# Halved norms of a two-block transformer kernel: narrower bank waits, another bank order, earlier evictions

## The reference

```
x = x + gt1 * mix                                           # "mix1"
x = x + gt2 * swiglu(modulate(x, norm2_g, sh2, sc2), ...)   # norm "n2", then "ffn1"
h = modulate_2(rmsnorm_2(x, g_ffn1), sh1, sc1)              # norm "nf1"
x = x + 0.5 * gt1 * swiglu_2(h, w_ffn1_in, w_ffn1_down)     # "ffn2"
proj = modulate_2(rmsnorm_2(x, g_mix), sh2, sc2) @ w_in     # norm "nm", then projections
x = x + gt2 * (y @ w_out)                                   # "mix2"
x = x + 0.5 * gt3 * swiglu_2(...)                           # norm "nf2", then "ffn3"
return rmsnorm_2(x, g_final)                                # norm "nfin"
```

## Time and profile before

| | us |
|---|---|
| median of 3 runs | 2013.97 (2013.62 to 2016.22) |
| the profiled execution | 2018.55 |
| its span, first to last instruction | 2016.7 |
| busy in the span: TensorE | 1956.7 (97%) |
| busy in the span: VectorE | 941.3 (47%) |
| busy in the span: ScalarE | 756.4 (38%) |
| busy in the span: GpSimd | 702.9 (35%) |

### The profile page before, as it was taken

How to read it: one execution, slowest core, us unless ns; L and a number is a source line. 1 busy time by engine, 2 the same in 40 slices (tenths; PEclk the granted TensorE clock), 3 DMA queues, 4 the chain that set the end, 5 groups by cost and what they waited for, 6 DMA issues and landing times.

```text
span 2016.7 us, 28119 instructions
## 1 busy us (share of the span) xinstructions
PE 1956.7 (97%) x11189; PEld 1572.3 (78%) x11189; DVE 941.3 (47%) x1465; ACT 756.4 (38%) x1298; POOL 702.9 (35%) x295
## 2 busy tenths in 40 slices
PE   7999999999999999999999999999999999999998
PEld 5788867888888888888888887656866788888886
DVE  2758668554444412544443255676875542323102
ACT  4553336543222213332221244445256442222212
POOL 1423301124444445244444523221421343444442
PEclk9989989999999999999999999999999999999999
DMA  7851100215444544244455522110311322333331
GB/s 315 301 208 43 48 7 22 84 50 167 146 137 148 183 134 140 76 154 146 135 172 187 172 72 78 46 53 22 94 43 32 94 85 94 94 95 103 94 94 63
DMA packets 61291, 223.38 MB, mean 111 GB/s; under 512 B 6928, under 2 KB 9232, under 8 KB 59536
## 3 DMA queue, kind: packets, MB, share of 16 engines
q1 hardware_dynamic: 60624, 219.70, 33.6%
q10 hardware_dynamic: 576, 2.43, 0.3%
HBM read 220.00 MB, written 2.10 MB: 110 GB/s over the span
## 4 chain that ended last, share of the span: by engine, by line
PE 88%; DVE 6%; ACT 2%; issue 2%; DMA 1%; SPq 0%; DVEq 0%; ACTq 0%
PE ps L450 77%; PE ps L1091 1%; DMA early_raw<-early 1%; DMA mod_w<-mod_w 1%; PE ps L1110 1%; DVE neg_max L1240 1%; PE ps L2539 1%; PE ps L2710 1%; PE ps L2731 1%; PE ps L1742 1%; PE ps L1101 0%; PE ps L2561 0%; PE ps L989 0%; PE ps L1011 0%; PE ps L2719 0%
## 5 line engine op out<-in xcount | busy, mean ns | idle before, releaser
L2119 POOL TENSOR_TENSOR w_lo<-raw,w_hi 128x1024 fp32r<-128x1024 f32 x262 | 635.5, 2426 | 1271.4 <-ACT w_hi L463 667.0
L450 PE MATMUL ps<-hh,w_hi 128*128 128x512 f32 (+1 forms) x1496 | 587.4, 393 | 8.5 <-DVE xT L1842 3.1
L450 PE MATMUL ps<-hl,w_hi 128*128 128x512 f32 (+1 forms) x1496 | 579.1, 387 | 0.0
L450 PE MATMUL ps<-hh,w_lo 128*128 128x512 f32 (+1 forms) x1496 | 578.8, 387 | 0.0
L450 PEld LDWEIGHTS ps<-hh,w_hi 128*128 128x128 f32 x1496 | 283.5, 190 | 74.9 <-issue 14.6
L450 PEld LDWEIGHTS ps<-hh,w_lo 128*128 128x128 f32 x1496 | 283.4, 189 | 58.1
L450 PEld LDWEIGHTS ps<-hl,w_hi 128*128 128x128 f32 x1496 | 283.7, 190 | 54.2
L2092 ACT ACTIVATE w_hi<-raw 128x1024 fp32r<-128x1024 f32 x126 | 133.7, 1061 | 469.5 <-PE ps L450 469.5
L516 DVE SCALAR_TENSOR_TENSOR mod_raw<-mod_raw,cond_ada 128x1024 f32<-128x1024 f32 x72 | 112.4, 1563 | 256.9 <-DMA mod_raw<-late 256.9
L450 PE MATMUL ps<-act_hi,w_hi 128*128 (+1 forms) x480 | 189.6, 395 | 0.0
L450 PE MATMUL ps<-act_hi,w_lo 128*128 (+1 forms) x480 | 189.6, 395 | 0.0
(11 more groups left out here) (494 smaller groups left out, 2691.6 us busy)
## 6 DMA issues: line engine op xcount, KB each, us to landing
raw<-stream SPq DMA_DIRECT2D x284, 512.0 KB, 3.6
mod_raw<-late SPq DMA_DIRECT2D x72, 512.0 KB, 4.6
early_raw<-early SPq DMA_DIRECT2D x32, 512.0 KB, 6.0
mod_w<-mod_w SPq DMA_DIRECT2D x8, 1024.0 KB, 20.1
xT<-xT SPq DMA_DIRECT2D x2, 1024.0 KB, 6.0
xT<-xT ACTq DMA_DIRECT2D x2, 1024.0 KB, 6.1
out<-fin SPq DMA_DIRECT2D x16, 128.0 KB, 1.9
cT<-cT SPq DMA_DIRECT2D x1, 1024.0 KB, 21.7
```

Source lines behind the costliest of these rows:

```text
L450: mm = pe.matmul(out, w, r, start=first and i == 0, stop=last and i == 2, skip_group_check=open_group)
L2119: pool.tensor_tensor(lo[:, :], raw[n % RING][:, :], hi[:, :].bitcast(F32), ALU.subtract)\
```

## The change

1. `ffn_tensor` no longer opens with waits for banks 0 to 3. Each of the first three slots waits for the release of its own bank, 0, 1 or 2, and the fourth product (bank 3) for bank 3's. All three waits still stand ahead of `first_products`.
2. `FFN_ORDER`, the order of the halved output chunks (and of the norm's chunks after them), puts chunk 0 second.
3. In `half_norm_vector` there is one more `chunks_until`, after `low`, with 13 + i.
4. In `proj2_tensor` the fourth product takes bank 3 instead of bank 1. Which bank all others take is unchanged.

```diff
-    FFN_ORDER = (4, 5, 6, 7, 0, 1, 2, 3)
+    FFN_ORDER = (4, 0, 5, 6, 7, 1, 2, 3)
...
             for i in range(KD):
-                chunks_until(11 + 2 * i)
                 if shift is None:
+                    chunks_until(11 + 2 * i)
                     scale(h, i)
                     continue
+                chunks_until(11 + 2 * i)
                 low(h, i)
+                chunks_until(13 + i)
                 if i + 2 < KD:
                     scale(h, i + 2)
...
     def ffn_tensor(pe, key, behind, name_in, name_out):
-        for b in range(4):
-            pe.wait_ge(*bank_freed[b])
+        freed = bank_freed[:4]
...
             pe.wait_ge(spent(n)[0], spent(n)[1] + it)
-            pe.wait_ge(bank_empty(b), it + f["empty0"][b])
+            if peeled:
+                pe.wait_ge(*freed[b])
+            else:
+                pe.wait_ge(bank_empty(b), it + f["empty0"][b])
...
         for u in range(3):
             pe.wait_ge(*spent(n0 + u))
-            pe.wait_ge(bank_empty(u), f["empty0"][u])
+            pe.wait_ge(*freed[u])
         first_products(pe, behind, [(u, g0 + u) for u in range(3)])
...
-            b = i % 2 if i != 2 else 2
+            b = i if i < 4 else i % 2
```

## The result

| | before | after |
|---|---|---|
| median (lowest to highest, 5 runs each, in turn on one chip), us | 2013.97 (2013.62 to 2016.63) | 2003.11 (1999.73 to 2004.64) |
| the profiled execution, us | 2018.55 | 2001.16 |
| its span, us | 2016.7 | 1999.4 |
| its mean granted clock of TensorE | 0.984 | 0.992 |

The ratio is 0.9938, with a 95% interval of 0.9924 to 0.9953. The change makes the kernel faster, as forecast.

A forecast was written before the change was run, and what follows sets the result against it. TensorE, busy 97% of the span, was taken to bound the kernel, so only its idle could be won. 1.86 + 1.85 + 1.22 + 1.68 = 6.61 us, from 2013.97 to 2007.4 us, range 2005.4 to 2010.1.

The forecast's parts named there:

- the five waits: At the boundaries: four TensorE waits for L1842, 6.4 us together, and one of 0.5 us for `wkr`; all the change can reach.
- Mix1 to ffn1: Boundary before ffn1: TensorE no longer waits for bank 3 and starts at 433.30 instead of 435.16, gain 1.86 us.
- Ffn1 to ffn2: Boundary before ffn2: no wait for bank 3 (1.30 us earlier), plus an earlier seventh eviction; gain 1.85 us in all.
- Ffn2 to the projections: Moved eviction starts the projections 0.51 us earlier; fourth product no longer waits for `wkr`'s eviction, 0.71 us; together 1.22 us.
- Mix2 to ffn3: Boundary before ffn3: bank 3's eviction no longer holds TensorE, which starts at 1636.78 instead of 1638.46, gain 1.68 us.
- A: Early starts run into their inputs at three boundaries, 1.5 us go: gain 5.1, time 2008.9 us; chance 0.10.
- B: The projections give their 1.22 us back in another wait: gain 5.4, time 2008.6 us; chance 0.06.
- the narrow margin of 0.2 us for the squares: At mix1, the sum of squares falls due at 435.46 and the last square ends at 435.30: the narrowest place.
- Rival D: Boundary pauses hide instruction fetches, up to 12.9 us, time 2020.3 us; chance 0.03 at full price, slower.
- Rival E: The moved evictions before ffn2 and the projections come no earlier, 0.55 and 0.51 us missing: 5.5, time 2008.4; chance 0.08.
- I take the sum from the median: Whole kernel: the 6.6 us of boundary gains subtracted from the median of 2013.97 us, giving 2007.4 us.
- Rival C: In the projections, a shifted start may add lower-clock time (2010.7 us, chance 0.07, within 0.2%) or equally lose a stretch (2005).

The follow-up runs named there:

- e3: The kernel before with only the bank waits of ffn_tensor narrowed: 2010.47 us, ratio 0.9967.
- e4: The kernel before with the new chunk order, the moved eviction and bank 3 for the fourth projection product, bank waits kept: 2012.21 us, ratio 0.9976.
- e6: The kernel before with TensorE made to wait for a later step of the norm at all four boundaries: 2031.04 us, ratio 1.0078.
- f3: The kernel with the longer pauses of e6, with unused matmuls ahead of that wait: 2020.67 us, ratio 1.003.
- with tail or head: The changed kernel with its last output stored twice (2006.38 us, 0.9956), or with SyncE waiting for its first transfer before issuing the next (2007.3 us, 0.9959).
- e1: The kernel before, unchanged, run again beside the kernel before: 2015.39 us, ratio 0.999.
- e9: The kernel before with its last output stored twice and waited for: 2016.44 us, ratio 1.0009.
- e10: The kernel before with SyncE waiting for its first transfer before it issues the next: 2016.19 us, ratio 1.0008.
- e7: The kernel before with its boundary pauses filled by unused matmuls, waits unchanged: 2012.73 us, ratio 0.9987.
- f1: The kernel before with its boundary pauses filled by unused matmuls, measured again: 2012.66 us, ratio 0.9989.

## Why the prediction was wrong, point by point

**What bounds the kernel, and the five waits: right.** The waits for L1842 are two of 0.37 us, that for `wkr` is gone, and the FFNs between the norms are the same to 0.01 us.

**Mix1 to ffn1: right.** Forecast 1.86 us earlier; 4.24 - 2.35 = 1.89. TensorE itself came last, not the first `low`: the start is 0.13 us behind the last product.

**Ffn1 to ffn2: right.** Forecast 1.85; 4.79 - 2.89 = 1.90. The split into 1.30 for the waits and 0.55 for the moved eviction is borne out by e3 (1.38), and e4 adds that the second is worth 0.14 by itself. The eviction stands where it was put, 0.39 us behind the `low`. The changed order cost nothing and won nothing, as costed.

**Ffn2 to the projections: right.** 0.51 forecast, 0.52 measured; for the fourth product 0.71 and 0.71 (0.12 us behind its predecessor instead of 0.83).

**Mix2 to ffn3: right.** 1.68 forecast, 1.69 measured.

**Rivals A and B fell.** From the start to the second spread it is 8.14 us at ffn2 both before and after (12.93 - 4.79 and 11.03 - 2.89), at ffn1 8.09 and 8.01: the narrow margin of 0.2 us for the squares held. (The prediction has 8.3 us for this stretch, because the times of the earlier trace rows lie 0.16 and 0.17 us behind the spreads' own starts, 813.21 and 1181.88; the comparison that it drew stands.) The projections give nothing back: the time at equal clock is short by 7.3 +- 0.5 us, not by 5.4.

**Rival D fell.** No boundary shows an idle put to issue. The window of ffn1 after is as full as in the earlier trace rows:

```profile
434.41:787.80 353.39, 353.39 (x1622) 292.72 (x1624) 128.22 (x137) 101.67 (x130) 157.72 (x66) 1.00 0.46 147
```

The fetch at a taken branch outside the fetched pages, of which the Trainium skill speaks (Runtime: NRT & Kernel Launch, section "Instruction fetch mechanics"), is not seen here, with the pause in front of it or without. Whether the targets of these branches lay outside the fetched pages no run shows.

**Rival E fell:** the moved evictions came when forecast.

**The step that failed: "the boundaries don't depend on what made that difference, so I take the sum from the median".** The boundaries indeed took no part in that difference of the first profile, but the clock depends on the boundaries. I took a pause at its length, and the sum has no term for the clock. The sum of lengths was right (6.61; 6.9 in rows, 7.3 +- 0.5 at equal clock), and the kernel won 11.3 +- 1.3 us over all its executions. The other 4.0 us are a mean clock of 0.9893 instead of 0.9861, or 13 us less at the lower level (43 instead of 56 per execution). Filling the pauses alone, with no start any earlier, wins 3.0 +- 1.7 us of the same kind.

Rival C saw that the lower clock comes after TensorE idled, and came near the size (2005 for a stretch won). Two things in it were wrong. It put the gain into the projections, as something that a shifted start may meet or miss, not at the boundaries, where the change removes the idle itself. And so it called gain and loss equally likely, where less idle speaks for a gain; the list of chances even has one for the loss (0.07) and none for the gain. That its 2005 lies near the measured time is in part luck. My range ended at one stretch won, 2 us taken off, and so short of C's own 2005. The trace of before could not have settled it: its four boundaries all stand at clock 1.00. The row that shows the mechanism came with a second profile of the same kernel.

**What is shown and what is open.** Shown: idle of TensorE at these boundaries can bring the clock down (e6 against f3, with pauses of 3.5 to 4.4 us), and filling the pauses of the kernel before, 0.9 to 2.3 us long, wins 3.0 +- 1.7 us with no start any earlier. Measured too: the changed kernel has a higher clock in its twenty-two executions, and with tail or head. Open: how the 4 us divide, and where in the program they are won. Of the four profiles with before's pauses (before, e1, e9, e10) one alone shows a fall of the clock at a boundary, worth 1.56 us in that place, or 0.4 us per profile; that is less than the 3 us per execution by which the filling wins. (e9 has a pause as long there, 2.35 us, without a fall.) Most stretches of lower clock lie in the first section and the projections, and they move from execution to execution (first sections of 423.7 to 435.7 us in the same code). On average over these four profiles and the six without the pauses, the projections are 2.6 us shorter without them (beyond the 0.71 us of the fourth product), and the first section 2.5 us. The first section stands ahead of every pause in question, so no pause of the same execution can have made that; ten profiles are too few to tell it from chance, and whether one execution leaves something behind for the next no run here asks. A rest of chance is in the 4 us as well: the first five executions of the changed kernel had a mean clock of 0.991, the next seventeen 0.9888.

## What to carry to other kernels

Price a pause of TensorE at its length and, on top, at what the clock can lose behind it, and let the range reach further to that side: here 6.6 us of earlier starts came with 11 us of time. Record the granted clock with every run and compare kernels at equal clock too, since a median of three can be 3 us off while the distance at equal clock is good to 0.5 to 1 us with 6 to 24 executions; and profile the kernel before twice before you trust its rows on where the clock stands. Where a wait for a bank is made narrower, put it ahead of the bank's first use; here that is worth half a microsecond more, by the rows alone.

## What the runs showed of the hardware that I had not expected

- Behind a pause of 2.3 us in the middle of full stretches TensorE's clock fell from 1.00 to a window mean of 0.66 in one profile (e1), and behind pauses of 2.25 to 2.35 us at the same place in three others it did not (before, e9, e10); pauses 2 to 3.5 us longer brought it down at all four boundaries of the one profiled execution (e6). The Trainium skill (TensorE: Matmul & The Clock Gate, section "A second HAM failure mode: psum-queue depth-cycling") says that short idles between groups of matmuls, if they are frequent enough, can make the clock swing between its two levels; the traces agree as to the swing, and show it with single pauses too, hundreds of microseconds apart.
- Matmuls that compute nothing, put where TensorE would wait, make the kernel 3.0 +- 1.7 us faster (e7 and f1) and take 10.2 +- 4.0 us off the kernel with long pauses (f3 against e6).
- Times of one kernel from 2009.3 to 2021.9 us are mostly its clock: with 1.25 us per 0.001 the scatter shrinks from 3.0 us (standard deviation) to 1.05 us.
